# Three modulation rows in the first block, from half pieces; two left in the expert stage

## The reference, cut to what matters

```python
def first_block(x, ...):
    h = rmsnorm(x, g_norm1)
    proj = h @ w_in                     # c_q, c_kv, k_pe, z_sgu, gates
    o_a = mla_branch(...)               # latent attention, 16 heads
    o_b = sgu_branch(z_sgu, ...)        # layer norm and mixing over tokens
    merged = gates_a * o_a + gates_b * o_b
    x = x + merged @ w_out
    x = x + peer_ffn(rmsnorm(x, g_norm2), ...)   # 16384 experts, all computed
    return rmsnorm(x, g_final)

def second_block(x, c, ..., w_mod, b_mod, ...):
    mod = jax.nn.silu(c) @ w_mod + b_mod         # 2048 x (6 * 2048)
    sh1, sc1, g1, sh2, sc2, g2 = jnp.split(mod, 6)
    h = rms_norm(x, norm1_g) * (1 + sc1) + sh1
    ...                                          # attention, state space, out
    x = x + g1 * (merged @ w_out)
    h2 = rms_norm(x, norm2_g) * (1 + sc2) + sh2
    ...                                          # convolution, feed forward
    return x + g2 * ((silu(gt) * val) @ w_down)
```

## Time and profile before

| | |
|---|---|
| median of 3 runs | 3509.93 us (3509.6 to 3512.47) |
| span of the profiled execution | 3507.9 us |
| the median beside this span | 2.0 us more |
| TensorE busy, products | 3493.6 us, 17108 |
| weight loads of TensorE busy | 2936.1 us (84%) |
| VectorE busy | 2663.4 us (76%) |
| ScalarE busy | 1914.7 us (55%) |
| GpSimd busy | 138.1 us (4%) |
| chain that ended last | TensorE 97%, VectorE 1%, ScalarE 1%, DMA 1% |
| granted TensorE clock | 1.000 |
| moved | 834.45 MB, 238 GB/s |

### The profile page before, as it was taken

One profiled execution on the slowest core, in us unless ns is written; L12 is line 12 of the kernel. 1 busy time (PEld: TensorE's weight loads), 2 busy tenths in 40 slices (PEclk: granted clock), 3 DMA queues, 4 the chain that ended last, 5 costly groups with the idle time before them and its releaser, 6 DMA issues.

```text
span 3507.9 us, 48487 instructions
## 1 busy us (share of the span) xinstructions
PE 3493.6 (100%) x17108; PEld 2936.1 (84%) x17108; DVE 2663.4 (76%) x3571; ACT 1914.7 (55%) x2468; POOL 138.1 (4%) x189
## 2 busy tenths in 40 slices
PE   9999999999999999999999999999999999999999
PEld 7898888888888888888888888878888888888887
DVE  6654557679888878888888888899976667667668
ACT  6554444555588864444444446557754555555544
POOL 2100000000000000000000001010000000000000
PEclk9999999999999999999999999999999999999999
DMA  8546658966667799999999997665566566666664
GB/s 282 184 157 200 194 178 285 302 227 216 215 221 260 256 334 355 323 328 327 340 339 336 339 343 214 188 183 165 166 183 217 184 191 187 191 191 185 192 191 144
DMA packets 279611, 834.45 MB, mean 238 GB/s; under 512 B 96481, under 2 KB 97121, under 8 KB 265105
## 3 DMA queue, kind: packets, MB, share of 16 engines
q1 hardware_dynamic: 250352, 660.69, 59.6%
q10 hardware_dynamic: 15120, 102.84, 7.6%
q0 software_dynamic: 13968, 68.64, 5.3%
HBM read 773.72 MB, written 39.87 MB: 232 GB/s over the span
## 4 chain that ended last, share of the span: by engine, by line
PE 97%; DVE 1%; ACT 1%; DMA 1%; issue 0%; SPq 0%; POOL 0%; DVEq 0%; ACTq 0%
PE ps L2643 25%; PE ps L2644 25%; PE ps L2645 25%; PE ps L3273 9%; PE ps L3277 5%; PE ps L2736 1%; PE ps L2737 1%; PE ps L2738 1%; PE ps L2989 1%; PE ps L2751 1%; DMA raw<-in_peer_v 1%; PE ps L3115 0%; PE ps L2686 0%; DVE lo L1483 0%; ACT hi L786 0%
## 5 line engine op out<-in xcount | busy, mean ns | idle before, releaser
L786 ACT CAST hi<-raw 128x1024 fp32r<-128x1024 f32 (+1 forms) x1215 | 1273.3, 1049 | 1440.8 <-PE ps L2645 1226.4
L1483 DVE TENSOR_TENSOR lo<-raw,hi 128x1024 fp32r<-128x1024 f32 (+1 forms) x1213 | 1470.6, 1220 | 759.3 <-ACT hi L786 757.9
L2643 PE MATMUL ps<-hi,xx 128*128 128x512 f32 x2176 | 859.0, 395 | 0.5 <-DVE lo L1483 0.5
L2644 PE MATMUL ps<-lo,xx 128*128 128x512 f32 x2176 | 848.0, 390 | 0.0
L2645 PE MATMUL ps<-hi,xx 128*128 128x512 f32 x2176 | 847.6, 390 | 0.0
L2643 PEld LDWEIGHTS ps<-hi,xx 128*128 128x128 f32 x2176 | 409.0, 188 | 87.7 <-issue 6.0
L2645 PEld LDWEIGHTS ps<-hi,xx 128*128 128x128 f32 x2176 | 408.6, 188 | 86.6
L2644 PEld LDWEIGHTS ps<-lo,xx 128*128 128x128 f32 x2176 | 409.2, 188 | 80.5
L2643 PE MATMUL ps<-hi,Ph 128*128 128x512 f32 x1020 | 397.4, 390 | 0.2 <-DVE X L1991 0.2
L2645 PE MATMUL ps<-hi,Pl 128*128 128x512 f32 x1020 | 396.9, 389 | 0.0
L2644 PE MATMUL ps<-lo,Ph 128*128 128x512 f32 x1020 | 396.8, 389 | 0.0
(11 more groups left out here) (514 smaller groups left out, 3921.7 us busy)
## 6 DMA issues: line engine op xcount, KB each, us to landing
raw<-in_peer_u SPq DMA_DIRECT2D x256, 512.0 KB, 4.3
raw<-in_peer_v SPq DMA_DIRECT2D x256, 512.0 KB, 6.5
mraw<-in_w_mod ACTq DMA_DIRECT2D x96, 1024.0 KB, 8.0
raw<-in_w_up SPq DMA_DIRECT2D x176, 512.0 KB, 3.7
raw<-in_w_in SPq DMA_DIRECT2D x143, 512.0 KB, 3.6
raw<-in_in SPq DMA_DIRECT2D x128, 512.0 KB, 3.6
raw<-in_w_down SPq DMA_DIRECT2D x88, 512.0 KB, 4.0
raw<-in_out SPq DMA_DIRECT2D x64, 512.0 KB, 4.3
```

The source lines that it names most:

```text
L786: SC.copy(hi[:, n0 % SPL, 0:w], raw[:, n0 % RAW, 0:w]).then_inc(hi_ready, 1)
L1483: V.tensor_tensor(lo[:, n0 % SPL, 0:w], raw[:, n0 % RAW, 0:w], hi[:, n0 % SPL, 0:w].bitcast(F32), ALU.subtract).then_inc(lo_ready, 1)
L2643: PE_.matmul(acc, xhi[:, k0 + k, xs], H, start=s0, stop=False)
L2644: PE_.matmul(acc, xhi[:, k0 + k, xs], L, start=False, stop=False)
```

## The change: what it does

Rows 0, 1 and 2 are worked out in the first block. `w_mod`'s pieces 0 to 47 are cut in halves of 128x1024. The halves lie where X lies (`mraw3`, two of them, 8 KB; beside them `cS3`, silu(c) broadcast, 8 KB). A half piece belongs to every second tile of 33 to 79 (24), to tiles of zv and zu but each sixth (54) and to three of four tiles in gb's first three chunks (18): 96. ScalarE issues the load of the next half right behind the cast (`early_next`), after the half before the current one is used (`mod3_used`); VectorE works the half out right behind the subtraction and ahead of what else belongs to the tile (`early_unit`). The sums go to `mpart`, where the convolution's columns used to lie, and are added up in "out".

x is therefore loaded a second time, on POOL's queue, when all halves are used; the columns of the convolution are loaded in the second block. In the expert loop no piece is left. `mod_late` holds rows 3 and 4, 32 pieces; it falls away in the last three and a half steps of the stage.

```diff
+EARLY_TILES = ([BASE["gm"] + n for n in range(TC + 4 * TL, 4 * (TC + 4 * TL), 2)]
+               + [BASE["zv"] + n for n in range(8 * TC) if n % 32 % 6 != 5]
+               + [BASE["gb"] + n for n in range(3 * TC) if n % 4 != 3])
+        cS3 = at("cS3", [P, D], 96)
+        mraw3 = at("mraw3", [P, 2, D // 2], 104)
+        mpart = at("mpart", [P, EARLY_ROWS * KD, 2], 112 + 4.5 + COFF["conv"] * 4 / 1024)
...
 # POOL
-            pool.dma_start(cols[:, COFF["conv"]:NCOLS], A["cols"][:, COFF["conv"]:NCOLS]).then_inc(late_in, 16)
...
+            pool.wait_ge(row_st, 16)
+            pool.wait_ge(sq_ready, 2)
+            pool.dma_start(cS3[:], crow.partition_broadcast(P)).then_inc(c_in, 16)
             pool.wait_ge(coef_ok, 2)
...
+            pool.wait_ge(mod3_used, EARLY)
+            pool.dma_start(X[:].rearrange("p t n -> p (t n)"), A["x"].rearrange("p t n -> p (t n)")).then_inc(sgu_in, 16)
             pool.wait_ge(merged_ok, 4)
...
 # ScalarE
+            def early_load(h):
+                act.dma_start(mraw3[:, h % 2], A["w_mod"][h // 2][:, h % 2 * (D // 2):h % 2 * (D // 2) + D // 2]
+                              ).then_inc(mod_in[h % 2], 16)
+            def early_next(n):
+                h = EARLY_AT.get(n, 0)
+                if 1 <= h < EARLY - 1:
+                    act.wait_ge(mod3_used, h)
+                    early_load(h + 1)
...
                     split(n0 + SPL + j)
+                    early_next(n0 + j)
...
 # VectorE
+            def early_unit(n):
+                h = EARLY_AT.get(n)
+                if h is None:
+                    return
+                if h == 0:
+                    dve.wait_ge(c_in, 16)
+                dve.wait_ge(mod_in[h % 2], 16 * (h // 2 + 1))
+                V.scalar_tensor_tensor(mraw3[:, h % 2], mraw3[:, h % 2], 1.0, cS3[:, h % 2 * (D // 2):...],
...
                     split(n0 + SPL + j)
+                    early_unit(n0 + j)
                     if r:
                         heads(r - 1, j)
...
 # VectorE, out
+                        if c == 0 and j in (0, 1):
+                            rows = mcol[:, 0:EARLY_ROWS].rearrange("p a k -> p (a k)")
+                            ...
                     dve.wait_ge(tile_used, n + TC)
+                    dve.wait_ge(sgu_in, 48)
...
 # expert loop, VectorE (and its loads on ScalarE)
-                        mod_unit(4 * i + j, rr)
...
             def mod_late(u):
+                if u >= LATE_ROWS * KD:
+                    return
```

More of the change, by code:

```diff
@@ L133 @@
 TURN3 = {8: 0, 9: 1, 10: 2, 11: 3, 13: 4, 14: 5}
+EARLY_TILES = ([BASE["gm"] + n for n in range(TC + 4 * TL, 4 * (TC + 4 * TL), 2)]
+               + [BASE["zv"] + n for n in range(8 * TC) if n % 32 % 6 != 5]
+               + [BASE["gb"] + n for n in range(3 * TC) if n % 4 != 3])
+EARLY_AT = {n: h for h, n in enumerate(EARLY_TILES)}
+EARLY = len(EARLY_TILES)
+assert EARLY == 2 * EARLY_ROWS * KD
 class Steps:
@@ L388, in build @@
         v_out = sem("v_out")
-        mod_in = [sem(f"mod_in{i}") for i in range(4)]
+        mod_in = [sem(f"mod_in{i}") for i in range(2)]
         mod_used, pow_ok = sem("mod_used"), sem("pow_ok")
         mod2_in, mod2_used = sem("mod2_in"), sem("mod2_used")
+        mod3_used = sem("mod3_used")
         csil, c_in = sem("csil"), sem("c_in")
@@ L922, in _ @@
                 n0, use = BASE["gm"] + (TC + 4 * TL) * r, 2 + 5 * r
+                if r == 1:
+                    act.wait_ge(sq_ready, 2)
+                    early_load(0)
+                    early_load(1)
                 for j in range(TC):
                     split(n0 + SPL + j)
+                    early_next(n0 + j)
                     if r:
@@ L1642, in gate_sum @@
                                            row, ALU.mult, ALU.add).then_inc(acc_free[use % 2], 1)
+            def early_unit(n):
[5 more added lines that the diff above has]
+                dve.wait_ge(mod_in[h % 2], 16 * (h // 2 + 1))
+                V.scalar_tensor_tensor(mraw3[:, h % 2], mraw3[:, h % 2], 1.0, cS3[:, h % 2 * (D // 2):h % 2 * (D // 2) + D // 2],
+                                       ALU.mult, ALU.mult, accum_out=mpart[:, h // 2, h % 2:h % 2 + 1]).then_inc(mod3_used, 1)
             split(BASE["kpe"] + SPL)
@@ L1781, in _ @@
                         split(n + SPL + j)
+                        if c == 0 and j in (0, 1):
+                            rows = mcol[:, 0:EARLY_ROWS].rearrange("p a k -> p (a k)")
+                            if j == 0:
+                                dve.wait_ge(mod3_used, EARLY)
+                                st.step(V.tensor_tensor(rows, mpart[:, :, 0], mpart[:, :, 1], ALU.add))
+                            else:
+                                st.wait()
+                                V.tensor_tensor(rows, rows, C("bmod", 0, EARLY_ROWS * KD), ALU.add).then_inc(mod_col, 1)
                         if c == 0 and j in (2, 3):
@@ L2008, in _ @@
                         v_add(v, c, off + (n + 10 + 2 * c))
[L2009 to L2013, removed]
             n0 += 16 * MAIN
-            dve.wait_ge(mod_col, PARTS + 1)
+            dve.wait_ge(mod_col, 2)
             V.scalar_tensor_tensor(mcol[:, 1], mcol[:, 1], 1.0, C("g3", 0, KD), ALU.add, ALU.mult).then_inc(mcol_ok, 1)
             def mod_late(u):
-                row, part = mraw[:, u % 2], PARTS + u // KD
-                dve.wait_ge(mod_in[u % 2], 64 * PARTS + 16 * (u // 2 + 1))
+                if u >= LATE_ROWS * KD:
+                    return
+                row, part = mraw[:, u % 2], EARLY_ROWS + u // KD
+                dve.wait_ge(mod_in[u % 2], 16 * (EARLY // 2 + u // 2 + 1))
                 V.scalar_tensor_tensor(row, row, 1.0, cS[:], ALU.mult, ALU.mult,
@@ L2574, in _ @@
             dve.wait_ge(zeroed, 2)
+            dve.wait_ge(late_in, 32)
             with dve.Fori(1, FB - 1) as b:
```

52 lines of the change are left out of this document (23 added, 29 removed).

## The result

| | before | after |
|---|---|---|
| median | 3510.73 us (11 runs, 3509.6 to 3555.32) | 3546.76 us (11 runs, 3542.82 to 3561.17) |
| ratio to before, 95% interval | | 1.0098 (1.008 to 1.0116) |
| span of the profiled execution | 3507.9 us | 3541.4 us |
| chain that ended last | TensorE 97%, DMA 1% | TensorE 90%, VectorE 4%, DMA 3% |

The change makes the kernel 36 us (1.0%) slower, where 7.6 had been forecast (3517.5 against 3509.9). Lines have moved with the edit: 1483 (the split) is now 1511, 1565 (gating) 1593, 1609 (a head's scaling) 1637, 1744 and 1745 (merge) 1787 and 1788, 2643 the first of a tile's products 2687, 2686 (turn) 2730, 2771 (values) 2815, 2859 (mixing) 2903. Piece halves are line 1680, their loads 930.

What follows compares the result with a forecast made beforehand. TensorE was taken to bound the kernel, nearly without gaps. 5.25 + 1.15 + 1.85 - 0.65 = 7.6 us on the 3507.9 span gives 3515.5, plus 2.0 to the median: 3517.5, range 3510.5 to 3526.

Steps and rivals of the forecast that it cites:

- First, second and third place: TensorE waits for VectorE: attention heads in three rounds (1.75 us each, 5.25), second mixing product (1.15), merged tiles' first turn (1.85).
- rival A: Rounds, mixing and merge have more play than the timeline shows, so pieces cost nothing there: 3509.3 us, chance 0.15.
- The transfers: In zv and zu a half piece lands in 4.3 us, at most 4.8, so two buffers keep TensorE's pace.
- The keep-up limit: In zv and zu two buffers keep pace up to 5.4 us of landing, about 5.0 with VectorE's other work.
- Rival B: Half pieces take 6 us to land in zv and zu, too slow for TensorE's pace: 11 us more, 3529, chance 0.18.
- a lead of 5.9 us: A split tile is ready some 5.9 us before TensorE wants it, so a single piece disappears in it.
- Given back: Expert stage without the moved pieces: 0.25 us at the loop's start, 0.4 at the stage's end, 0.65 in all.
- The XG wait: TensorE's wait for XG at the expert stage's end: from 1.1 us, shrinking by 0.4, to near 0.7.
- What I cost at nothing: Remaining pieces, ScalarE's loads and waits, silu(c) broadcast, reload of x, row additions, moved columns: all covered, no cost.

Runs made afterwards that it cites:

- experiment 1: Changed kernel with 94 of the 96 half-piece loads left out, all 96 pieces still worked out on VectorE: 3517.33 us, ratio 1.002.
- experiment 2: Changed kernel with four half buffers for two, loads three pieces ahead, weights multiplied by themselves instead of silu(c): 3517.09 us, ratio 1.0015.
- experiment 9: Changed kernel with three half buffers for two, loads two ahead, weights multiplied by themselves instead of silu(c): 3517.3 us, ratio 1.0021.
- Experiment 7: Changed kernel with 94 of 96 half-piece loads left out and each piece placed behind the other work of its tile: 3511.68 us, ratio 0.9997.
- experiment 5: Changed kernel with pieces cut to 32 columns on VectorE, all 96 loads and two buffers kept: 3519.93 us, ratio 1.0013.
- experiment 4: Changed kernel without 94 of the 96 half pieces and their loads; two-row expert stage and second load of x stay: 3508.57 us, ratio 0.9993.
- experiment 8: Changed kernel, nothing left out: pieces behind other work, two more half buffers for part of the way, last seven halves on every second tile: 3512.87 us, ratio 1.0006.
- experiment 3: Changed kernel with each piece placed behind VectorE's other work at its tile, loads and two buffers unchanged: 3534.72 us, ratio 1.0068.
- experiment 6: Changed kernel with halves read from contiguous tiles of w_in instead of half rows of w_mod: 3539.23 us, ratio 1.0079.

## Why the prediction was wrong, by its steps

**Direction right, size wrong.** Slower was forecast, at 3517.5; it is 3546.8. The forecast's 3517.5 is the time of the kernel without the cost of its loads: experiments 1, 2 and 9 gave 3517.3, 3517.1 and 3517.3. That it fits to 0.4 us is in part luck: the places cost 8.6 us where 8.25 were summed, and experiment 1's span shows 1.0 given back where 0.65 was.

**First, second and third place: right.** The earlier trace rows with the piece set in is, in the changed kernel's timelines of VectorE and TensorE in round 2:

```profile
195.04 1.22 DVE L1511 TENSOR_TENSOR lo<-raw,hi 128x1024 fp32r<-128x1024 f32 x1 [0.64 <-ACT hi L802]
...
196.18 1.22 DVE L1680 SCALAR_TENSOR_TENSOR mraw<-mraw,cS 128x1024 f32<-128x1024 f32 x1
...
197.52 0.61 DVE L1637 SCALAR_TENSOR_TENSOR GM<-ps,stat,GM 128x128 f32<-128x128 f32 x2
...
198.27 0.46 PE L2815 MATMUL ps<-vv,pT 128*128 128x128 f32 x2 [1.03 <-DVE GM L1637]
```

Split, piece, scaling, and TensorE 1.03 us late, where 1.0 had been said. A round is 1.9 us longer (1.14 and 0.75 at its two stands), not 1.75. Experiment 7 shows that it is the place in VectorE's order that counts: the same pieces behind these results cost 5.6 us less, and that falsifies rival A, which held that VectorE was not what the places go by.

**The transfers: the step that failed,** in the words "I take 4.3 (between the two, since the two queues' loads are issued about 2 us apart)". The upper bound of 4.8 was the mistake. It came from the earlier trace rows: one load alone, plus the other's 1.2 us on top. That is the price of one meeting. In the changed kernel a half took 5.3 us in the median, and 5.6 between 410 and 465 us. With TensorE kept at its pace the same 0.5 MB took 6.4 to 6.7 us between 330 and 410 us (experiments 2, 5 and 9), 1.8 times the 3.6, and 5.6 to 6.1 from there to 465. My reading is that the loads hardly ever stand alone at this demand and each waits behind what both queues have outstanding; no run shows the queues' inside. With 5.6 and a piece of 1.2 two buffers turn in 6.8 us, with 6.4 in 7.6, where 6.5 are allowed. The keep-up limit itself (5.0 to 5.4 us) was about right: the changed kernel's medians are at it (5.3 and 5.6), and it loses where the loads are over it (5.1 to 7.0 in the chain's rows).

By the Trainium skill's limit of about 358 GB/s per core (DMA: Bandwidth & Descriptors, Specifications), which I had weighed there, there would have been no room either, but the trace disagrees with that: 399 and 408 GB/s passed for 40 us without a stand in experiment 2. The Trainium skill (HBM Reference, Specifications) also says that a core streaming alone measures about 425 GB/s; the trace agrees, with 424 in the earlier trace rows. I was right not to go by 358, and wrong to conclude from a rate that was free that the landing time was short. They are two questions.

**Rival B had the mechanism and too small a price.** It gave 6 us of landing and 11 us; the loads cost 29.4 by the medians, 25.9 by the spans. Three things were missing from it. First, it counted the 64 tiles of zv and zu with a lead of 5.9 us to be used up; that lead was used up once (0.5 us in tiles 81 to 113), but behind it tiles 113 to 133 grew by 8.4. Second, results without any lead take a late landing as a whole: the mixing product's wait is 8.2 against 1.4 with the landing covered, the turn's 3.7 against 1.5. Third, TensorE's clock fell around three of the stands: 5.95 in place of 3.69 us for the mixing products, 2.4 us more for tile 160, and a stretch of 3.4 us at the lower level behind the split's 2.43. The waits of the list make 15.2 of the 25.6 us by which the changed kernel's table exceeds experiment 1's (8.2 - 1.4, 6.2 and 3.7 - 1.5). The lower clock makes about 7.0 of the other 10.4, by an estimate: half of the 3.4, 4.6 and 6.0 us in which products ran at the lower level. The last 3.4 would be stands that modelled ends hide; no row separates them. The profiled execution, at the low end of the runs' spread, may have lost less than the median one.

**Given back: right in kind, small.** 0.65 was said, the span of experiment 4 shows 1.4: by the starts of its tiles 0.5 at the beginning of the expert loop (0.25 had been said), 0.4 at the end of the stage and 0.3 at tile 842, which no term had. The XG wait is 0.8, 0.7 had been said.

**What I cost at nothing** held otherwise: with the landing covered, no stretch but the three places grew (experiments 1, 2 and 9), so the reload of x was hidden, the broadcast (experiment 1, the only one of the three that has it) and ScalarE's 96 issues (experiments 2 and 9). One item of that list had a condition: a wait for `mod3_used` was to keep ScalarE's next cast back "only while VectorE is late anyway". In the changed kernel VectorE is late, and ScalarE stood 30 times at that wait, 73.9 us in all (6 times and 10.5 us in experiment 2). What this adds to the loss, beside the landing itself, is not shown: no run issues the halves from a queue that carries no casts.

## What to carry to other kernels

When a ring of loads is put beside a stream that already runs, check its period and not the rate: landing time plus work, divided by the number of buffers, against the pace, with a landing time of 1.6 to 1.8 times the lone one, as it was here, and not the lone one plus one transfer. Take one buffer more than the sum asks for before anything else; here 4 KB of each partition were worth 29 us of the 36. And filler work on an engine that runs in order belongs behind the results that the bottleneck waits for at that tile, not behind the first instruction of the tile: it was worth 5.6 us, and moving two pieces by one tile took off the last 2.3 us of the rounds.

## What the runs showed of the hardware

- Two queues with 0.5 MB loads: 3.6 us to landing with one of them, 5.3 where the second is held up by its ring, 6.4 to 6.7 where both keep near TensorE's pace (361 and 375 GB/s between 330 and 410 us in experiments 5 and 2, 408 over 20 us), 5.6 in experiment 2 at 352 GB/s (410 to 465 us); with three buffers 6.7 and 5.9 in these two windows, with four 6.6 and 5.6. Beside two rows of 1 MB, three halves issued within 1.4 us took 9.6 to 13.8 (experiment 8).
- Source rows of 4 KB out of 8 KB against contiguous tiles: 5.3 against 4.8 us over all 96 loads, 5.3 in both between 330 and 410 us.
- TensorE's granted clock fell at stands of 2.4, 3.7 and 8.2 us of an otherwise full engine (0.93, 0.87 and 0.81 of full over 25 us with each), and products then started 0.43 us apart, near twice 0.23: the lower of its two levels. It did so as well at 3.0 and 5.4 us (experiment 3), 4.1 (experiment 5), and 2.9 and 6.9 (experiment 6). At the stands of 1.0 to 1.7 us of experiments 1, 2, 3 and 6 it did not; the mixing products of experiments 1 and 2 took 3.69 us.
